# Rotary scores as pairs of 64-row tiles, two attention steps at a time, and a later load of the query latent weights, in an eight-core decoder layer

## What is computed

```python
h = rmsnorm(x, g_pre)
c_q, c_kv, k_rope = h @ w_in[...]                     # 512, 512 and 64 columns
q = (rmsnorm(c_q, q_norm_g) @ w_uq)                   # per head: 128 "nope" + 64 rotary
q = concat(q_nope, apply_rope(q_pe, cos, sin))
kv = (rmsnorm(c_kv, kv_norm_g) @ w_ukv)               # per head: k_nope 128, v 128
k = concat(k_nope, apply_rope(k_rope, cos, sin))      # the rotary key is shared by all heads
s = (q @ k.T) * 192**-0.5                             # causal
o = softmax(s) @ v
# apply_rope: [t1*cos - t2*sin, t2*cos + t1*sin]
```

## Time and profile before

| | us |
|---|---|
| median of the 3 runs | 3221.74 |
| lowest and highest run | 3221.01, 3522.28 |
| the profiled execution's own time | 3221.04 |
| span of its slowest core (core 6) | 3219.3 |
| spans of the eight cores | 3212.6 to 3219.3 |
| attention, first to last score matmul | 417.9 to about 1691 |

### The profile page before, as it was taken

One profiled execution on the slowest core, in us unless ns is written; L12 is line 12 of the kernel. 1 busy time (PEld: TensorE's weight loads), 2 busy tenths in 40 slices (PEclk: granted clock), 3 DMA queues, 4 the chain that ended last, 5 costly groups with the idle time before them and its releaser, 6 DMA issues.

```text
span 3219.3 us, 61465 instructions; the slowest of 8 cores (3212.6 to 3219.3 us)
## 1 busy us (share of the span) xinstructions
PE 3116.9 (97%) x25001; PEld 1929.2 (60%) x25408; DVE 1162.3 (36%) x2230; ACT 1028.9 (32%) x1227; POOL 153.3 (5%) x292
## 2 busy tenths in 40 slices
PE   5999999999999999999999999999999999999998
PEld 3555577777777777777785545444444444444444
DVE  5444454444444444444442003316133111111114
ACT  3565444444444444444452112111110000000012
POOL 1000000000000000000001110000000000000010
PEclk8999999999999999999999999999999999999999
DMA  9645300000000000000046785255443444444485
GB/s 161 100 86 99 70 8 15 15 15 15 15 15 8 8 8 8 8 8 8 2 104 107 134 148 98 46 86 95 76 79 66 79 76 75 79 73 78 79 165 169
DMA packets 49811, 208.08 MB, mean 65 GB/s; under 512 B 5888, under 2 KB 6016, under 8 KB 46336
## 3 DMA queue, kind: packets, MB, share of 16 engines
q0 software_dynamic: 41472, 174.15, 31.6%
q1 hardware_dynamic: 8064, 29.99, 2.9%
HBM read 369.85 MB, written 8.39 MB: 117 GB/s over the span
## 4 chain that ended last, share of the span: by engine, by line
PE 90%; DVE 4%; issue 3%; ACT 2%; DMA 2%; POOL 0%; DVEq 0%; SPq 0%; ACTq 0%; POOLq 0%
PE ps L312 24%; PE ps L1368 10%; PE ps L830 8%; PE ps L788 7%; PE ps L794 7%; PE ps L764 7%; PE ps L744 7%; PE ps L1245 3%; PE ps L517 3%; PE ps L1420 3%; PE ps L1152 2%; PE ps L715 1%; DMA AR<-xaT 1%; PE ps L1125 1%; PE ps L1049 1%
## 5 line engine op out<-in xcount | busy, mean ns | idle before, releaser
L806 ACT ACTIVATE AR<-ps 128x768 bf16<-128x768 f32 (+1 forms) x656 | 603.0, 919 | 669.2 <-PE ps L794 596.3
L312 PE MATMUL ps<-AR 128*128 128x512 bf16 x3502 | 780.7, 379 | 4.7 <-issue 0.4
L312 PEld LDWEIGHTS ps<-AR 128*128 128x128 bf16 x3584 | 350.4, 98 | 418.8 <-issue 2.2
L830 PE MATMUL ps<-AR 128*128 128x129 bf16 x4608 | 373.4, 221 | 7.9 <-DVE AR L769 5.2
L788 PE MATMUL ps<-AR 128*128 128x256 bf16 (+2 forms) x2176 | 358.7, 279 | 1.8 <-DVE AR L730 0.9
L794 PE MATMUL ps<-AR 128*128 128x256 bf16 (+2 forms) x2176 | 358.5, 279 | 0.0
L830 PEld LDWEIGHTS ps<-AR 128*128 128x128 bf16 x4608 | 303.7, 98 | 73.4 <-issue 10.3
L1368 PE MATMUL ps<-AR 128*128 128x512 bf16 x1506 | 340.0, 381 | 1.7 <-issue 0.2
L764 PE MATMUL ps<-AR 128*128 128x128 bf16 x4096 | 290.2, 220 | 4.4 <-DVE AR L585 3.7
L764 PEld LDWEIGHTS ps<-AR 128*128 128x128 bf16 x4096 | 260.0, 98 | 56.7 <-issue 6.7
L517 PE MATMUL ps<-AR 128*128 128x512 bf16 x964 | 262.4, 397 | 19.1 <-DVE AR L439 13.5
(11 more groups left out here) (155 smaller groups left out, 2291.7 us busy)
## 6 DMA issues: line engine op xcount, KB each, us to landing
AR<-wts POOLq DMA_DIRECT2D x256, 512.0 KB, 5.1
AR<-xaT POOLq DMA_DIRECT2D x14, 2048.0 KB, 16.1
AR<-xoT SPq DMA_DIRECT2D x16, 512.0 KB, 4.6
AR<-xo SPq DMA_DIRECT2D x8, 1024.0 KB, 9.3
y<-AR SPq DMA_DIRECT2D x16, 512.0 KB, 4.8
AR<-xaT POOLq DMA_DIRECT2D x8, 512.0 KB, 31.6
AR<-rows SPq DMA_DIRECT2D x12, 256.0 KB, 6.2
AR<-wcA POOLq DMA_DIRECT2D x4, 576.0 KB, 18.0
```

Source lines behind the costliest of these rows:

```text
L312: ins = h.matmul(ps[:, out_pair_b + half, :], w3[:, k, :], act3(k)[:, half * 512:(half + 1) * 512], start=(k == 0), stop=(k == 15))
L806: sc.add("act", lambda h: h.activation(out=pT[pt][:, :, 0:w], in_=ps[:, sb:sb + 2, 0:w], func=AF.Exp), reads=pregs(sb), writes=(("pT", pt),))
L830: ins = h.matmul(ps[:, ob, o:o + 129], pT[pt][:, r, i * n + (j - s["jl"]) * 128:i * n + (j - s["jl"] + 1) * 128], vaug[:, kb, :], start=(k ...
```

## The change

1. In stage one the 2 MB load of `wcq` moves on POOL's queue from before tile 2's x to behind it, and the 16 DVE operations that scale `wcq` by `g_pre` move from between tiles 1 and 2 into tile 2, directly ahead of the query matmuls. From tile 2 on each quarter of the squares is written one block earlier.
2. `emit_qr` now does the rotation itself: ACT copies and scales the 128x512 result into `rt0`, DVE multiplies each 64-row half by its table, adds them, and writes the sum twice, to partitions 0 to 63 and 64 to 127 of `qr`.
3. `emit_qk2` replaces `emit_qk`. It takes two steps. First come the rotary scores of both steps, as 64x128 tiles: the even key block of a pair in rows 0 to 63 of the array, the odd one in rows 64 to 127, each into its own PSUM bank. Then the nope scores of the first step, its exponential, the nope scores of the second, its exponential. The steps are walked in 328 pairs: scores of the next pair, minima of this pair, then for each of its two steps filling and values product.
4. `rt0` stands where `hT(7)` will stand and `rt1` where `stg` buffer 9 stood. So only 7 pieces of `xoT` come early, all through buffer 8, and buffer 9 moves to 28 KB, in the middle of `ckvn`.

```diff
@@ first stage
-    sc.dma("pool", lambda h, sem: h.dma_start(out=wcq[:, :, :], in_=wcQ_d[:, :, :]).then_inc(sem, 16), "wcQ", 1, writes=("wcQ",))
...
             for b in range(4):
-                if b > 0:
-                    sc.add("act", lambda h, b=b: h.activation(out=sq[:, 4 * b:4 * b + 4, :], in_=xt[:, 4 * b:4 * b + 4, :], func=AF.Square),
-                           reads=(("xa", xb_, b),), writes=(("sq", b),))
+                for q in ((1,), (2,), (3,), ())[b]:
+                    sc.add("act", lambda h, q=q: h.activation(out=sq[:, 4 * q:4 * q + 4, :], in_=xt[:, 4 * q:4 * q + 4, :], func=AF.Square),
+                           reads=(("xa", xb_, q),), writes=(("sq", q),))
                 accs = [(b, 0)] + ([(4, 1)] if own and b == (3 if u == NQ_ else 0) else [])
                 for slot, is_q in accs:
+                    if is_q and u == NQ_:
+                        scale_w(range(16), wcq, "wcQ")
...
-        if u == 1:
-            scale_w(range(16), wcq, "wcQ")
+        if u == 0:
+            sc.dma("pool", lambda h, sem: h.dma_start(out=wcq[:, :, :], in_=wcQ_d[:, :, :]).then_inc(sem, 16), "wcQ", 1, writes=("wcQ",))
@@ emit_qr
-        sc.add("dve", lambda h: h.scalar_tensor_tensor(out=qr[hd % 2][:, hs], in0=ps[:, b, :], scalar=QSC, in1=Tq[:, hs], op0=ALU.mult, op1=ALU.mult),
-               reads=pregs(b, 1) + ("Tq0", "Tq1"), writes=(("qr", hd % 2, hs.start),))
+        o = qr[hd % 2]
+        n = hs.start
+        sc.add("act", lambda h: h.activation(out=rt0, in_=ps[:, b, :], func=AF.Copy, scale=QSC), reads=pregs(b, 1), writes=("rt0",))
+        sc.add("dve", lambda h: h.tensor_tensor(out=rt1[0:64, :], in0=rt0[64:128, :], in1=Tq[64:128, hs], op=ALU.mult), reads=("rt0", "Tq1"), writes=("rt1",))
+        sc.add("dve", lambda h: h.tensor_tensor(out=rt0[0:64, :], in0=rt0[0:64, :], in1=Tq[0:64, hs], op=ALU.mult), reads=("rt0", "Tq0"), writes=("rt0",))
+        for p0 in (0, 64):
+            sc.add("dve", lambda h, p0=p0: h.tensor_tensor(out=o[p0:p0 + 64, hs], in0=rt0[0:64, :], in1=rt1[0:64, :], op=ALU.add),
+                   reads=("rt0", "rt1"), writes=(("qr", hd % 2, n),))
@@ emit_qk2 (new)
+        def fn(h):
+            for s in pair_:
+                sb, n, c0, c1 = s["sb"], s["n"], s["jl"] * 128, (s["jb"] + 1) * 128
+                r_ = qr[s["hd"] % 2]
+                for i, ke in enumerate(s["kes"]):
+                    for r in range(2):
+                        kb = ke + r
+                        h.matmul(ps[:, sb + r, i * n:(i + 1) * n], kpe2[r * 64:r * 64 + 64, kb * 128:(kb + 1) * 128],
+                                 r_[r * 64:r * 64 + 64, c0:c1], start=(i == 0), stop=False, skip_group_check=True)
+            return nope(h, pair_[0])
...
+        sc.add("pe", fn, reads=tuple(rd), writes=tuple(q for s in pair_ for q in pregs(s["sb"])))
+        emit_exp(pair_[0])
+        sc.add("pe", lambda h: nope(h, pair_[1]), reads=tuple(rd), writes=pregs(pair_[1]["sb"]))
+        emit_exp(pair_[1])
@@ buffers of the next stage
-    STG_KB = [32 + 4 * i for i in range(8)] + [137, 141]
+    STG_KB = [32 + 4 * i for i in range(8)] + [137, 28]
...
-        i = 8 + k % 2 if k < 8 else k - 8
+        i = (8 if k < 7 else 9) if k < 8 else k - 8
...
-    NEARLY = 8
+    NEARLY = 7
@@ main loop
-        if g + 1 < len(all_steps):
-            emit_qk(all_steps[g + 1])
-            emit_exp(all_steps[g + 1])
-        emit_min(s)
...
+    pairs = [(all_steps[q], all_steps[q + 1]) for q in range(0, len(all_steps), 2)]
+    emit_qk2(pairs[0])
+    for pi_, pr in enumerate(pairs):
+        if pi_ + 1 < len(pairs):
+            emit_qk2(pairs[pi_ + 1])
+        for s in pr:
+            emit_min(s)
+        for s in pr:
...
```

More of the change, by code:

```diff
@@ L799, in emit_qk, with emit_qk2, nope @@
                writes=pregs(sb))
+    def emit_qk2(pair_):
+        for s in pair_:
+            s["sb"] = 2 * rot("sb", 2)
+        def fn(h):
+            for s in pair_:
+                sb, n, c0, c1 = s["sb"], s["n"], s["jl"] * 128, (s["jb"] + 1) * 128
[6 more added lines that the diff above has]
+            return nope(h, pair_[0])
+        def nope(h, s):
+            ins = None
+            if True:
+                sb, n, c0, c1 = s["sb"], s["n"], s["jl"] * 128, (s["jb"] + 1) * 128
+                q_ = qn[s["hd"] % 2]
+                for i, ke in enumerate(s["kes"]):
+                    for r in range(2):
+                        kb = ke + r
+                        ins = h.matmul(ps[:, sb + r, i * n:(i + 1) * n], kT[:, kb * 128:(kb + 1) * 128], q_[:, c0:c1],
+                                       start=False, stop=True, skip_group_check=True)
+            return ins
+        rd = {}
+        for s in pair_:
+            for ke in s["kes"]:
+                rd[("kT", ke // 4)] = rd[("kpe2", ke // 4)] = None
+            for o in (0, 512):
+                rd[("qn", s["hd"] % 2, o)] = rd[("qr", s["hd"] % 2, o)] = None
+        sc.add("pe", fn, reads=tuple(rd), writes=tuple(q for s in pair_ for q in pregs(s["sb"])))
+        emit_exp(pair_[0])
+        sc.add("pe", lambda h: nope(h, pair_[1]), reads=tuple(rd), writes=pregs(pair_[1]["sb"]))
+        emit_exp(pair_[1])
     def emit_exp(s):
@@ new lines, in build @@
+    pairs = [(all_steps[q], all_steps[q + 1]) for q in range(0, len(all_steps), 2)]
[6 more added lines that the diff above has]
+        for s in pr:
+            i, hd = s["i"], s["hd"]
+            if i == n_ab and hd + 1 < NHEAD:
+                whn, wrn = head_weights()
+                fill = mixed(hd + 1, whn, wrn)
+                done, span_, base = 0, n_c, n_ab
+            elif i == 0:
+                if hd > 0:
+                    fill = []
+                    for t in range(6, 16):
+                        fill += tile_units(t, whn, wrn)
+                done, span_, base = 0, n_ab - 1, 0
+            if hd == NHEAD - 1:
+                if i == 0:
+                    wsz.prefetch(2)
+                if i == n_ab:
+                    for k in range(NEARLY, 16):
+                        load_stg(k)
+                    wsz.prefetch(NEARLY - 2)
+                    sc.dma("pool", lambda h, sem: h.dma_start(out=v2(189, 4096), in_=memT[:, :]).then_inc(sem, 16), "memn", 1, writes=("memn",))
+                if i >= n_ab + 5 and i - n_ab - 5 < 16 - NEARLY:
+                    scale_stg(NEARLY + i - n_ab - 5)
+            if hd == 0 and i >= 4 and i < 12:
+                sl = slice((i - 4) * 128, (i - 3) * 128)
+                sc.add("dve", lambda h, sl=sl: h.reciprocal(out=rstd_o[:, sl], in_=rstd_o[:, sl]), reads=("rstd_o",), writes=("rstd_o",))
+            if 1 <= hd < 1 + NEARLY:
+                if i == 0:
+                    load_stg(hd - 1)
+                if i == n_ab:
+                    scale_stg(hd - 1)
+            goal = min(len(fill), -(-len(fill) * (i - base + 1) // span_))
+            while done < goal:
+                fill[done]()
+                done += 1
+            if i == per_head - 1:
+                fill, done = [], 0
+            if s is pr[0] and pi_ in pend:
+                for un in pend.pop(pi_):
+                    un()
+            if pi_ + 1 == len(pairs) and s is pr[1]:
@@ L1033, in build @@
             if s["last"]:
-                pend[g + 2] = emit_final(s, ob)
+                pend.setdefault(pi_ + 1, []).append(emit_final(s, ob))
     for un in rest_z:
@@ L1037, in build @@
     for g in sorted(pend):
-        pend[g]()
+        for un in pend[g]:
+            un()
     def mem_k(c):
```

44 lines of the change are left out of this document (1 added, 43 removed).

## The result

| | before | changed |
|---|---|---|
| median of all 6 runs each | 3223.2 us | 3193.1 us |
| the same without the slow ones | 3221.9 us | 3192.1 us |
| ratio | 1 | 0.9896 (0.9868 to 0.9923) |
| profiled execution | 3221.0 us | 3190.0 us |
| first score to last filling, core 3 | 1252.4 us | 1228.5 us |

The account below looks back on a forecast made before the run. PE was taken to bound the kernel, the attention being a stream of columns without holes. From 3221.0 us, -125 + 54 + 7 + 4 + 6 - 6 - 5 = -65 gave 3156 us, range 3100 to 3240.

Parts of the forecast that it names:

- first stage: Before the attention: moving wcq's load and scaling gives -6 us (-12 to +3), squares sooner -5 us (-8 to 0).
- both buffers at once, end of last head: Attention: rotary block waits for both exponentials, +7 us (0 to 20); more late xoT loads at the end, +6 (0 to 12).
- rotation of the query: Query rotation, 32 times per run: one ACT and four DVE operations, mostly covered, +4 us (0 to 32).
- changes of shape: Attention: 656 switches of the array between 128x128 and 64x128, 82 ns each, +54 us (0 to 171).
- half tiles at once: Rotary scores: both halves of a pair stream fully at once, halving 250 us: -125 us (-125 to 0).
- I take half the passage, 82 ns: Price assumed per array shape change: half of the 163 ns a 128x256 matmul lasts beyond its stream time.
- rival of a full emptying: Attention: the engine empties at each shape change, 163 to 261 ns, total 3209 to 3273 us; chance 0.2.
- the cheap one: Attention: a shape change costs next to nothing, under 30 ns, total 3102 to 3122 us; chance 0.15.
- half of it is 0.61: Query rotation: a 512-column DVE product takes half of 1.23 us for 1024 columns, so four take 2.4 to 2.8 us.
- an end after 5 us was set against a need after 4.6: Query rotation: key copy ends about 5 us after the query matmul, its bank wanted after about 4.6.
- the limit of the pairs: Attention, rival: ACT limits the pairs of steps, 0.3 us for each of 328 pairs, 3254 us; chance 0.08.
- The rival of halves one after the other: Rotary scores: the second half tile starts only when the first has streamed, 3281 to 3334 us; chance 0.1.

Follow-up runs that it names:

- e1: Kernel before with only the first stage's edits (wcq load behind tile 2's x, its scaling ahead of the query matmuls, squares a block earlier): ratio 0.995.
- e4: e2 with the former query rotation, one DVE operation per half: ratio 0.9975 to the kernel before.
- e2: Changed kernel with full 128x128 rotary tiles in place of half tiles, query scaled by half: ratio 1.0058 to the kernel before.
- e3: Changed kernel with both rotary matmuls of a pair in rows 0 to 63, so they cannot overlap: ratio 1.0244 to the kernel before.
- e9: Changed kernel with the rotation's sine product and second sum on POOL, cosine product and first sum on DVE: ratio 0.9871 to the kernel before.
- e7: Changed kernel with the late xoT piece that goes to 28 KB issued fourth in place of first: 3186.6 us, ratio 0.9885 to the kernel before.
- e5: Changed kernel with rotary scores, nope scores and exponential one step at a time, 1312 changes of shape: 3244.8 us, ratio 1.0067 to the kernel before.
- e6: Changed kernel with the four DVE operations of the query rotation moved to POOL: 3187.3 us, ratio 0.9892 to the kernel before.

## Why the gain was half of the forecast

By its steps, in us; "ratios" and "medians" are the ladder before, e1, e4, e2, e3, changed kernel:

| step | forecast | ratios | medians | from |
|---|---|---|---|---|
| first stage | -11 | -16 | -16 | e1 |
| both buffers at once, end of last head | +7 +6 | +8 | +9 | e4 less e1 |
| rotation of the query | +4 | +27 | +25 | e2 less e4 |
| changes of shape | +54 | +60 | +60 | e3 less e2 |
| half tiles at once | -125 | -112 | -108 | changed less e3 |
| sum | -65 | -33 | -30 | |

Each step by ratios has some 10 us of uncertainty, that of two ratios, so the sum is closed on core 3's timelines too. From the distances between the starts of PE's matmuls, from the first score to the last filling, the stream time of these matmuls is taken off: columns over 2.4 GHz and 2.2 ns each, and 57.8 ns for one of the 129 columns of a values product, which is what they take in a row. What is left are the holes, waits and the loss at a lower clock alike. The window of before holds 16 matmuls less than the others, 1.3 us.

| core 3 | span, us | stream | holes |
|---|---|---|---|
| before | 1252.4 | 1241.9 | 10.5 |
| e4: in pairs | 1257.7 | 1243.2 | 14.5 |
| e2: and the new rotation | 1277.4 | 1243.2 | 34.2 |
| e3: and changes of shape | 1337.4 | 1243.2 | 94.2 |
| changed: and halves at once | 1228.5 | 1121.0 | 107.5 |

The change took 121 us of stream out and put 97 us of holes in: -24. Ahead of it the first score starts 9.6 sooner (415.6 to 406.0), behind it 5 us are lost: -28, and this core's span fell from 3216.9 to 3188.0. The steps one by one:

**Rotary scores as half tiles: right in the stream, 13 us short in the net.** -125 was forecast with both halves fully at once, and from e3 to the changed kernel the stream is 122 us shorter up to the last filling, half of what the rotary columns there take. The net of 108 to 112 is this less 13 us of holes that come back (94 to 107.5): the listed waits for key copies (L716 and L751) and of the transposes behind the values products (L896) total 4.8 us in this window in e3 and 18.0 in the changed kernel, because shorter score blocks cover less of DVE's work. In e9, with half of the rotation taken off DVE, they total 4.4. So these 13 us, too, hang on the rotation's place in DVE's queue. The Trainium skill (TensorE: Matmul & The Clock Gate, Measured speedup vs the span model) gives 3.07 times for four row tiles of 32 rows. Two of 64 rows gave 0.65 / 0.325 = 2.0 times here, without such a loss, once the changes of shape are counted apart.

**Changes of shape: the mechanism right, 54 forecast, 69 measured.** The step that failed is "I take half the passage, 82 ns". Against the same blocks of e2, in the 311 of 328 without a wait or a lower clock, the changed kernel needs 0.096 us more ahead of the rotary matmuls, 0.105 behind them and 0.010 at the first nope matmuls: 0.211 per pair of steps (0.208 to 0.214), 0.209 in e3, and 328 x 0.211 = 69. In the time it was 60, since in e3 it hid 7 us of listed waits (21.4 in e2, 14.3 in e3). The Trainium skill (TensorEngine Tiling (Array Packing), Key Properties) says that changing the mode drains the engine. The trace agrees that each change costs, at 105 ns, less than the 163 ns that a 128x256 matmul is under way beyond its stream time. So the rival of a full emptying, from 163 ns on, fell, and the cheap one (under 30) with it.

**Rotation of the query: the miss that decided, 4 forecast, 25 (medians) to 27 (ratios) measured.** Three parts of the step failed. First, "half of it is 0.61": DVE's timeline in head 13 of the changed kernel, core 3, with the ACT copy ahead and PE behind:

```profile
1409.35 0.60 ACT L733 ACTIVATE AR<-ps 128x512 f32<-128x512 f32 x1 [0.21 <-PE ps L716]
...
1410.05 0.69 DVE L734 TENSOR_TENSOR AR<-AR 64x512 f32<-64x512 f32 x1 [1.32 <-ACT AR L733]
...
1410.84 0.68 DVE L735 TENSOR_TENSOR AR<-AR 64x512 f32<-64x512 f32 x1
...
1411.62 1.47 DVE L737 TENSOR_TENSOR AR<-AR 64x512 bf16<-64x512 f32 x2
...
1413.13 0.69 DVE L755 CAST AR<-ps 128x512 bf16<-128x512 f32 x1
...
1413.97 0.59 PE L716 MATMUL ps<-AR 128*128 128x512 bf16 x2 [0.52 <-DVE AR L755]
```

The four take 1413.13 - 1410.05 = 3.1 us with the gaps between them, not 2.4 to 2.8. The key copy is ready at 1413.82 and PE could have gone on at about 1413.3. Second, the cover did not hold: an end after 5 us was set against a need after 4.6, which the rows bear out, but 4 us were booked for all of it. PE waits 15 times ahead of L716, 0.51 or 0.84 us each, and 8 times ahead of L751, 0.64 each, and the values matmuls (L771) wait 7 times for a bank that the ACT copy still reads. In e2, where the score blocks are longer, the first two are 0.3 to 0.6 us each, and the holes grew by 20 us, from 14.5 to 34.2. Third, an omission: the first head's query has no work ahead of it that could hide the rotation, 6.0 us where it was 0.9. 20 + 5 = 25.

Some of the 20 is clock. Behind the wait of 6.0 us the granted clock is 0.50, the 1.2 GHz level, until about 415 us; in e4, with a wait of 0.9, only for part of such a stretch. The columns are those of the earlier trace rows, the changed kernel first:

```profile
406.00:415.00 9.00, 6.59 (x27) 2.59 (x28) 1.24 (x5) 4.31 (x5) 0.00 (x0) 0.50 0.01 2
...
398.00:408.00 10.00, 7.08 (x50) 4.42 (x51) 1.86 (x7) 4.31 (x5) 0.00 (x0) 0.83 0.01 2
```

At half the clock the 6.59 busy us lose 3.3. In e4 a mean of 0.83 over 10 us is 3.4 us at half the clock, which lose 1.7.

The waits as listed in e2 are 19 us over those in e4 (13.5 from the first score to the last filling, 5.1 ahead of it). A listed wait begins when the last matmul is through, and the stream has stopped 0.16 us before: in the rows above PE idles 0.52 us, and the distance holds 0.68 too much. In the changed kernel 15 such waits, 10.0 us by the list, are 12.4 us of holes.

**Both score buffers at once, and the last head: 13 forecast, 8 to 9 measured, the mechanism as forecast.** The wait comes in 8 heads as foretold, at 0.42 us and not 0.8 (once 0.70); once, at the first pair, it is 2.4 to 2.7. In e4 these are 7.8 us of holes, near the 7 forecast. But the holes grew by 4 only, since the 15 waits of values matmuls for a copy (L830 for L769, 7.7 us of holes in the kernel before) went at the same time, which the step did not foresee. The end of the last head cost 5 where 6 was forecast. Its six waits of 0.7 to 0.9 us for both buffers cost nothing, as foretold: e7 kept them and lost the 5 us. ACT never became the limit of the pairs: PE waited for it at 15 of the 328.

**The first stage: -11 forecast, -16 measured (-9 to -23), its parts the other way round.** That the sum came near is luck. PE's timeline of the changed kernel at tile 2's query matmuls, core 3:

```profile
88.99 6.11 PE L514 MATMUL ps<-AR 128*128 128x512 bf16 x16 [8.10 <-DVE AR L423]
```

Start and idle time are close to the forecast's 87 and 8. But behind the pause the matmuls run at half the clock at first: 16 of 512 columns are 3.4 us at 2.4 GHz and took 6.1. Of the forecast 6 us, 2 or 3 were left. For the squares the step counted the listed waits, on one core and from 98 us on (7.4, on core 3 they are 9.0), took 5 of them, and left the clock out.

**The rival of halves one after the other** forecast 3281 to 3334. Built on purpose as e3 it gave 3302: its sum was right, its premise was not.

## What to carry to other kernels

A contraction over 64 rows, two of them side by side as row tiles, streams in half the time, but every stretch of such tiles cost 0.21 us here for going in and coming out, the time of 500 columns at 2.4 GHz: put many columns into one stretch. Per pair of steps it saved 0.33 to 0.44 us for 0.21; per single step (e5) the two nearly cancelled. Cost a moved operation at the queue that it joins and not by the engine's share: DVE was half idle, and yet four operations cost 25 us, most of it because a key copy behind them came some half a microsecond late again and again. In a stream without holes a wait costs more than the profile lists, here by 0.16 us each, and in stage one by what the granted clock lost with it.

## What the runs showed of the hardware that was not expected

- A change between 128x128 and 64x128 tiles costs 0.105 us on average, 0.211 for going in and coming out (0.208 to 0.214 in 311 blocks), around matmuls of 128, 256 and 384 columns, and about as much each when there are 1312 of them.
- Two 64-row tiles stream at twice the rate of one, their weight loads included: eight 128x256 matmuls in 0.55 - 0.11 = 0.44 us, in place of 0.87.
- A DVE product of 64x512 takes 0.686 us, more than half of the 1.226 for 128x1024, and as long as the operation on 128x512 that it replaced, 0.692. With the gap behind it one takes 0.78. On POOL it is 1.26 us.
- POOL's four operations held up DVE's minima on 128x256 (e6): the 22 minima that ran beside one took 872 ns in the median and up to 1302, the 166 others of the attention 291. DVE's copies out of PSUM (L755) took 690 to 692 ns beside them as without them. The 7 minima that ran beside POOL's operations in e9 took 281 to 283 ns, so it does not happen each time, and why is open.
- Waits of some tenths to three microseconds in stage one went together with a mean granted clock of 0.96, their absence with 1.00. Ahead of the attention a wait of 6.0 us went together with 1.2 GHz for the 9 us behind it.
